# A pooling mixer and a SwiGLU layer on one core: the first layer norm's gain and bias leave VectorE's full-row pass and enter by ScalarE's copies and a later pass over rows

## The chip, the cores and the metric

One core of a Trainium2 chip. The metric is the device time of one execution in microseconds; the median of several executions is compared.

## The reference, cut to what matters

2048 tokens plus 16 learned meta tokens, 1024 features, one layer. All arithmetic is in float32.

```
m = pool_mixer(h)                                   # trailing means over 2, 4, 8, 16 tokens, w_group, w_out
h = layer_norm(ALPHA * h + m, mix_g, mix_b)         # (x - mean) * rstd * g + b
h = layer_norm(ALPHA * h + swiglu(h), ffn_g, ffn_b) # 2816 hidden features
out = h[16:]
```

## The kernel before

**Precision.** Each matmul operand is split into a rounded part ("hi", a cast by ScalarE) and a remainder ("lo", a subtraction by VectorE), and each product is three matmuls: 12 matmuls of 128x512 for four feature tiles.

**Mixer.** Four blocks of 512 tokens. `mixer_block` takes 4 chunks of hidden products (L855) and 4 of outward products (L871). ScalarE copies each hidden pair from PSUM (`stage_u`, L1093), VectorE pools it, and ScalarE and VectorE split the result again. VectorE adds `ALPHA` times the rows to the outward products (`add_rows`), takes their statistics (`aggregate`, L1441), GpSimd raises the variance to the power -0.5 (`rstd_of`, L708), and VectorE applies the norm in two passes over each row tile of 128x1024 (`apply`, L1448 and L1453). The block's four row tiles `z[:, j]` are normed in the next block, those of the last block in units 1 and 2 of the next stage. SyncE then stores them to `h_dram` (`store_h`).

**Turning.** For the gate and up products the rows must have features in partitions. TensorE transposes pairs of row tiles (`turn_part`, L843), four 128x128 at a time into a PSUM bank, and ScalarE copies each bank to SBUF (`take_turn`, L1084). Four pairs are turned in block 2, four in units 5 to 16. GpSimd makes sums of them (`pair_sums`).

**Gate and up.** The products go by a scheme of seven products for eight (`product`, L1014). There are 44 units; units 0 to 21 work on the first half of the tokens and 22 to 43 on the second. A unit is seven products, 0 to 6, of 12 matmuls each. An order written out by hand puts the other engines' work between them. Three steps must be over before TensorE goes on:

- product 2 waits for ScalarE's copy of product 0 (`b_seeded`, L1297);
- product 4 waits for VectorE's sum, called the seed below (`c_seeded`, L1610). It needs product 2 and `s5`, ScalarE's copy of product 1 (L1306);
- product 6 waits for VectorE's sum L1643 (`c22_made`), which needs product 4.

In VectorE's order the seed of unit n stands behind three remainders for the weights of unit n + 1 (`unit_lo`, L1513), and the last of these waits for a cast (`unit_hi`, L1186) that stands in ScalarE's order behind the copy `s5`:

```
                dve.wait_ge(prod_done, NP * n + 3)
                dve.wait_ge(s5_taken, n + 1)
```

GpSimd makes four differences of each unit's weights (`unit_t123`, `unit_t4`), in even units from 24 on also four 128x1024 sums (`s_forms`, L769 and L704), and up to unit 28 forms of the down weights (`tform`).

**Down.** 56 products (L1043). VectorE's `take` adds each to `z0` or `z1`, which `load_hz` and `load_hs` fill with the stored rows. The rows get `ALPHA` in VectorE's first `take` (L1678) and in two multiplications by ScalarE (L1359, L1362). GpSimd adds two of the parts (L812, L816). The last layer norm and the stores follow.

Of the kernel before, what the change touches and what calls it, by code (L numbers as in the profile page):

```python
# [30 lines left out]
def trunk(nc, x, x_t, meta_t, w_in, w_group_t, scale, w_out, mix_g, mix_b, w_gu, w_down, ffn_g, ffn_b,  # L31
# [34 lines left out]
    with ExitStack() as ctx:  # L66
# [107 lines left out]
        hs_landed = [sem("hs_landed0"), sem("hs_landed1")]  # L174
        out_stored = sem("out_stored")
# [34 lines left out]
        rstd_ready = sem("rstd_ready")  # L210
        centered = sem("centered")
# [130 lines left out]


# [15 lines left out]
        def _(sp):  # L359
# [147 lines left out]

            def load_hs(m):
# [6 lines left out]
            def store_out(r):  # L515
                zz = z0 if r < MT else z1
                sp.wait_ge(ln_applied, BLOCKS * TT + r + 1)
                sp.dma_start(out_rows[:, r, :], zz[:, r % MT].rearrange("p h t -> p (h t)")).then_inc(out_stored, 16)

            def store_last_out():  # L520
                for h in range(2):
                    sp.wait_ge(ln_applied, BLOCKS * TT + 2 * MT + h)
# [23 lines left out]
            for n, v in enumerate((mix_g, mix_b)):  # L546
                sp.dma_start(gb[:, n, :], v.partition_broadcast(P)).then_inc(gb_landed, 16)
# [80 lines left out]
            for n in range(UNITS):  # L628
# [73 lines left out]
        def _(pool):  # L702
# [19 lines left out]
            def pair_sums(pi):  # L722
                st, ss = st_of(pi), ss_of(pi)
                pool.wait_ge(turn_taken, 4 * pi + 4)
# [57 lines left out]
            pool.wait_ge(half_ready, 1)  # L782
            rstd_of(0)
# [25 lines left out]
            for m in range(MT):  # L809
                pool.wait_ge(taken, taken_by(3, m))  # L810
                pool.wait_ge(h12_scaled, m + 1)
                nc.gpsimd.tensor_tensor(z0[:, m, 1, :], z0[:, m, 1, :], z1[:, m, 1, :], ALU.add).then_inc(h12_added, 1)  # L812
                pool.wait_ge(h2_scaled, m + 1)
# [9 lines left out]
        def _(pe):  # L823
# [5 lines left out]
            def turn_part(pi, k):  # L829

                part = TT * pi + k
                if k == 0 and pi < TT:
                    pe.wait_ge(h0_landed[pi], 16)
                    pe.wait_ge(ln_applied, TT + pi + 1)
# [3 lines left out]
                if pi < TT and part >= 2:  # L838
                    pe.wait_ge(turn_taken, part - 1)
                elif pi >= TT:  # L840
                    pe.wait_ge(turn_taken, part)
# [975 lines left out]
```

## Time and profile before

| | us |
|---|---|
| median of 3 runs (1675.25 to 1678.51) | 1675.52 |
| the profiled execution, its own time | 1677.79 |
| its span | 1676.0 |
| TensorE busy | 1662.2 (99%) |
| VectorE busy | 982.6 (59%) |
| ScalarE busy | 582.3 (35%) |
| GpSimd busy | 606.1 (36%) |
| mean share of the DMA engines | some 5 tenths, 182 GB/s |
| chain that ended last | TensorE 96%, VectorE 1%, issue 1%, DMA 1%, ScalarE 1% |

Engine busy times overlap. A row of a group of instructions tells how long they ran and how long their engine was idle just before them; a row of the waits tells for whom. TensorE's granted clock was at full speed (2.4 GHz) in nearly all of the 40 slices of the span.

### The profile page before, as it was taken

Reading aid. Unit: us, or ns where it says so; the run is one execution under the profiler, and the core shown is the slowest. Engines: PE = TensorE matmul, PEld = TensorE weight load, DVE = VectorE, ACT = ScalarE, POOL = GpSimd, SP = SyncE. Lnnn points to the kernel's source line nnn. Section 1 sums busy time; section 2 is a strip of 40 time slices with the busy share of each in tenths; the row PEclk is TensorE's granted clock in tenths of the full one; section 3 lists DMA queues with packets and bytes.
Section 4 is the critical chain, followed back from the end, with each engine's and each line's share of the span. In section 5 each row is a group of like instructions: output and inputs, shape, how many; then the busy total and the mean of one; then the engine's idle time right before and its main releaser. Section 6 shows DMA issues by size and latency. Waiting matters only on the chain.

```text
span 1676.0 us, 19024 instructions
## 1 busy us (share of the span) xinstructions
PE 1662.2 (99%) x7410; PEld 1374.1 (82%) x7410; DVE 982.6 (59%) x1057; ACT 582.3 (35%) x791; POOL 606.1 (36%) x414
## 2 busy tenths in 40 slices
PE   9999999999999999999999999999999999999998
PEld 7888888888888888888878888888888888888886
DVE  6658688787744445344655564454554443568866
ACT  5332334244333333333533333333343432332320
POOL 0000024104455566565257766666632000341002
PEclk9999999999999999999999999999999999999999
DMA  9534639654445455465435676444558443554542
GB/s 358 196 104 174 224 132 323 208 211 158 155 157 165 155 195 195 152 227 179 158 108 181 207 211 202 142 138 142 197 184 306 151 157 128 193 210 175 198 147 93
DMA packets 182410, 305.67 MB, mean 182 GB/s; under 512 B 7600, under 2 KB 131632, under 8 KB 172592
## 3 DMA queue, kind: packets, MB, share of 16 engines
q1 hardware_dynamic: 142624, 272.46, 47.9%
q10 hardware_dynamic: 37520, 23.60, 4.7%
q0 software_dynamic: 2176, 8.39, 1.3%
q8 instruction: 59, 0.97, 0.2%
q14 instruction: 31, 0.25, 0.0%
HBM read 216.86 MB, written 87.56 MB: 182 GB/s over the span
## 4 chain that ended last, share of the span: by engine, by line
PE 96%; DVE 1%; issue 1%; DMA 1%; ACT 1%; POOL 0%; SPq 0%; POOLq 0%; ACTq 0%; DVEq 0%
PE acc L1014 42%; PE acc L1043 18%; PE acc L871 10%; PE acc L855 10%; PE turn L1014 7%; PE turn L1043 5%; PE acc L908 1%; PE turn L843 1%; PE acc L921 1%; DMA raw<-w_out 0%; ACT fb L1173 0%; PE acc L933 0%; DMA hs<-h_dram 0%; DMA dwr<-w_down 0%; DVE dw L1584 0%
## 5 line engine op out<-in xcount | busy, mean ns | idle before, releaser
L1014 PE MATMUL acc<-fb,wf 128*128 128x512 f32 x1584 | 364.6, 390 | 2.5 <-DVE g L1643 2.5
L1014 PE MATMUL acc<-fa,wf 128*128 128x512 f32 x1584 | 366.1, 390 | 0.0
L1014 PEld LDWEIGHTS acc<-fb,wf 128*128 128x128 f32 x1584 | 298.4, 188 | 65.0 <-issue 2.9
L1014 PEld LDWEIGHTS acc<-fa,wf 128*128 128x128 f32 x1584 | 296.1, 188 | 61.2
L1043 PE MATMUL acc<-dw,da 128*128 128x512 f32 x1386 | 315.8, 389 | 0.3 <-DVE dw L1584 0.3
L1043 PEld LDWEIGHTS acc<-dw,da 128*128 128x128 f32 x1386 | 260.0, 188 | 55.0 <-DVE dw L1584 1.0
L1513 DVE TENSOR_TENSOR wf<-wt,wf 128x512 fp32r<-128x512 f32 x132 | 125.9, 955 | 178.4 <-ACT wf L1186 178.2
L1513 DVE TENSOR_TENSOR wf<-wr,wf 128x512 fp32r<-128x512 f32 x176 | 179.8, 1030 | 80.1 <-ACT wf L1186 79.6
L1186 ACT CAST wf<-wr 128x512 fp32r<-128x512 f32 x176 | 108.7, 618 | 233.1 <-PE acc L1014 220.6
L704 POOL TENSOR_TENSOR wt<-wr,wt 128x512 f32<-128x512 f32 x88 | 128.0, 1454 | 142.7 <-DVE wf L1513 141.6
L855 PE MATMUL acc<-mov,split 128*128 128x512 f32 x768 | 176.7, 390 | 0.0
L871 PE MATMUL acc<-split,act_sb 128*128 128x512 f32 x768 | 176.2, 390 | 0.0
L871 PEld LDWEIGHTS acc<-split,act_sb 128*128 128x128 f32 x768 | 143.7, 188 | 29.7
L855 PEld LDWEIGHTS acc<-mov,split 128*128 128x128 f32 x768 | 143.5, 188 | 29.5
L1578 DVE TENSOR_TENSOR da<-dar,da 128x1408 fp32r<-128x1408 f32 x56 | 92.1, 1644 | 119.4 <-ACT da L1270 119.4
L1270 ACT CAST da<-dar 128x1408 fp32r<-128x1408 f32 x56 | 76.9, 1372 | 183.9 <-PE acc L1043 146.1
L704 POOL TENSOR_TENSOR wt<-wr 128x512 f32<-128x512 f32 x44 | 58.9, 1339 | 152.5 <-DMA wr<-w_gu 124.1
L1043 PE MATMUL turn<-dw,da 128*128 128x512 f32 x462 | 105.9, 389 | 0.0
L1043 PEld LDWEIGHTS turn<-dw,da 128*128 128x128 f32 x462 | 86.7, 188 | 18.0
L1186 ACT CAST wf<-wt 128x512 fp32r<-128x512 f32 x132 | 81.9, 621 | 52.8 <-PE acc L1014 37.5
L1374 DVE TENSOR_TENSOR split<-raw,split 128x2048 fp32r<-128x2048 f32 x31 | 72.5, 2338 | 38.9 <-ACT split L1063 38.9
L1063 ACT CAST split<-raw 128x2048 fp32r<-128x2048 f32 x31 | 59.4, 1915 | 95.3 <-PE acc L871 92.0
(115 smaller groups left out, 1588.4 us busy)
## 6 DMA issues: line engine op xcount, KB each, us to landing
wr<-w_gu SPq DMA_DIRECT2D x44, 1024.0 KB, 4.9
dar<-af_dram SPq DMA_DIRECT2D x56, 704.0 KB, 4.5
af_dram<-g ACTq DMA_DIRECT2D x33, 512.0 KB, 3.7
raw<-fold_dram SPq DMA_DIRECT2D x16, 1024.0 KB, 5.6
raw<-w_in SPq DMA_DIRECT2D x15, 1024.0 KB, 6.2
fs<-hf_dram SPq DMA_DIRECT2D x14, 1024.0 KB, 6.7
dt_raw<-w_down SPq DMA_DIRECT2D x22, 512.0 KB, 6.2
wt_dram<-dt_t SPq DMA_DIRECT2D x22, 512.0 KB, 3.6
```

The costliest lines, as they stand in the source:

```text
L704: return nc.gpsimd.tensor_tensor(out_, a, b, ALU.subtract)
L843: mm = nc.tensor.transpose(turn[:, slot, n * P:(n + 1) * P], pair_rows(pi, a)[:, kk * P:(kk + 1) * P], ident[:])
L855: mm = nc.tensor.matmul(acc[:, 2 * banks + m, :], w[:, a, k, m * P:(m + 1) * P], mov[:, k, v, :], start=k == 0 and n3 == 0, stop=k == KT - ...
L871: mm = nc.tensor.matmul(acc[:, OUT_BANK[half][j], :], act_sb[:, k0 + k, v, j * P:(j + 1) * P], w[:, a, k, :], start=first and k == 0 and n ...
L1014: mm = nc.tensor.matmul(dst, wf[:, slot, a, k, :], fa[half][i][:, v, :, k, :], start=i < 2 and k == 0 and n3 == 0, stop=k == KC - 1 and n3 ...
L1043: mm = nc.tensor.matmul(down_bank(k), da[k % 3][:, v, p, :], dw[:, slot, a, :], start=p == 0 and n3 == 0, stop=p == JF - 1 and n3 == 2)
L1063: nc.scalar.copy(split[:, slot, 0, 0:kn], raw_of(c, slot)[:, 0:kn]).then_inc(w_hi_ready, 1)
L1186: nc.scalar.copy(wf[:, (NP * n + i) % 8, 0].rearrange("p k n -> p (k n)"), w_source(n, i)).then_inc(wf_hi, 1)
L1270: nc.scalar.copy(da[k % 3][:, 0], dar[:, k % 2]).then_inc(da_hi, 1)
L1374: nc.vector.tensor_tensor(split[:, slot, 1, 0:kn], raw_of(c, slot)[:, 0:kn], f32(split[:, slot, 0, 0:kn]), ALU.subtract).then_inc(w_lo_rea ...
L1513: nc.vector.tensor_tensor(wf[:, s, 1].rearrange("p k n -> p (k n)"), w_source(n, i), f32(wf[:, s, 0]).rearrange("p k n -> p (k n)"), ALU.s ...
L1578: nc.vector.tensor_tensor(da[k % 3][:, 1], dar[:, k % 2], f32(da[k % 3][:, 0]), ALU.subtract).then_inc(da_lo, 1)
```

## The change

- `aggregate` and `rstd_of` stay. GpSimd takes two more small steps per block: mean times rstd, and its negative, `shift`.
- `apply` is gone. ScalarE writes `z * rstd + shift` in one pass for each row tile (`norm`): at the beginning of the next block, and for the last block two tiles behind `s5` in unit 1 and two in unit 2. `h_dram` now holds rows without gain and bias.
- `take_turn` brings them in: features lie in partitions there, so `mix_g` and `mix_b` are a scale and a bias per partition. One copy of 128x512 becomes two activations of 128x256.
- The stored rows are finished in units 24 to 39, one row tile of 128x1024 in each: SyncE loads it (`load_row`), VectorE multiplies by `ALPHA * g` and adds `ALPHA * b` (`finish_h`), SyncE stores it back (`store_row`). ScalarE scales the two broadcast vectors once, 128x2048, behind `s5` in unit 24.
- `ALPHA` is then in the stored rows: the two multiplications by ScalarE in the down stage go, and the first `take` is a plain addition.

```diff
@@ load_tform @@
-                else:
-                    sp.wait_ge(ln_applied, BLOCKS * TT)
@@ SyncE @@
+            def load_mgb():
+                sp.wait_ge(fa_lo, 2 * NP)
+                for n, v in enumerate((mix_g, mix_b)):
+                    sp.dma_start(mgb[:, n, :], v.partition_broadcast(P)).then_inc(mgb_landed, 16)
+            def load_row(r):
+                if r >= len(rows):
+                    sp.wait_ge(row_final, 16 * (r - 1))
+                n = r % len(rows)
+                sp.dma_start(rows[n][:], h_rows[:, r, :]).then_inc(row_landed[n], 16)
+            def store_row(r):
+                sp.wait_ge(row_ready, r + 1)
+                sp.dma_start(h_rows[:, r, :], rows[r % len(rows)][:]).then_inc(row_final, 16)
...
+                if n == ROW_UNIT0 - 1:
+                    load_mgb()
+                if 0 <= n - ROW_UNIT0 + 1 < 2 * MT:
+                    load_row(n - ROW_UNIT0 + 1)
+                if 0 <= n - ROW_UNIT0 < 2 * MT:
+                    store_row(n - ROW_UNIT0)
                 if n == UP_LAST - 3:
+                    sp.wait_ge(row_final, 16 * 2 * MT)
                     load_dw(0, 0)
@@ GpSimd, rstd_of @@
                 nc.gpsimd.tensor_tensor(rstd[:, 0:TT], var_eps[:, 0:TT], minus_half[:], ALU.pow).then_inc(rstd_ready, 1)
+                pool.wait_ge(rstd_ready, s + 1)
+                nc.gpsimd.tensor_tensor(mean_rstd[:], mv[:, 0:TT, 0], rstd[:, 0:TT], ALU.mult).then_inc(mean_scaled, 1)
+                pool.wait_ge(mean_scaled, s + 1)
+                sub(shift[:], zeros[:], mean_rstd[:]).then_inc(shift_ready, 1)
@@ ScalarE, take_turn @@
-                nc.scalar.copy(st_of(pi)[:, :, k, :], turn[:, slot, :].rearrange("p (b t) -> p b t", t=P)
-                               ).then_inc(turn_taken, 1)
+                for n, kk in enumerate((k, KC + k)):
+                    nc.scalar.activation(st_of(pi)[:, 2 * n:2 * n + 2, k, :],
+                                         turn[:, slot, 2 * n * P:2 * (n + 1) * P].rearrange("p (b t) -> p b t", t=P),
+                                         ACT.Identity, bias=mix_b_sb[:, kk:kk + 1], scale=mix_g_sb[:, kk:kk + 1]
+                                         ).then_inc(turn_taken, 1)
@@ ScalarE, mixer_block and units @@
+            def norm(s, j):
+                if j == 0:
+                    act.wait_ge(shift_ready, s + 1)
+                nc.scalar.activation(z[:, j, :], z[:, j, :], ACT.Identity, bias=shift[:, j:j + 1],
+                                     scale=rstd[:, j:j + 1]).then_inc(normed, 1)
...
+                    if b:
+                        for j in ((0, 1), (2,), (3,), ())[i]:
+                            norm(b - 1, j)
...
                 nc.scalar.copy(s5[:], bank_d).then_inc(s5_taken, 1)
+                if n == ROW_UNIT0:
+                    act.wait_ge(mgb_landed, 32)
+                    nc.scalar.mul(mgb[:], mgb[:], ALPHA).then_inc(mgb_scaled, 1)
+                if n in (1, 2):
+                    norm(LAST, 2 * (n - 1))
+                    norm(LAST, 2 * (n - 1) + 1)
@@ ScalarE, down stage @@
-                    nc.scalar.mul(z0[:, m, 1, :], z0[:, m, 1, :], ALPHA).then_inc(h12_scaled, 1)
-                    nc.scalar.mul(hs[:, m % 2], hs[:, m % 2], ALPHA).then_inc(h2_scaled, 1)
@@ VectorE @@
-            def apply(s, j):
...
-                nc.vector.scalar_tensor_tensor(out=z[:, j, :], in0=z[:, j, :], scalar=mv[:, j, 0:1], in1=gb[:, 0, :],
-                                               op0=ALU.subtract, op1=ALU.mult).then_inc(centered, 1)
...
-                nc.vector.scalar_tensor_tensor(out=z[:, j, :], in0=z[:, j, :], scalar=rstd[:, j:j + 1], in1=gb[:, 1, :],
-                                               op0=ALU.mult, op1=ALU.add).then_inc(ln_applied, 1)
+            def finish_h(r):
+                if r == 0:
+                    dve.wait_ge(mgb_scaled, 1)
+                n = r % len(rows)
+                dve.wait_ge(row_landed[n], 16 * (r // len(rows) + 1))
+                nc.vector.tensor_tensor(rows[n][:], rows[n][:], mgb[:, 0, :], ALU.mult).then_inc(row_gained, 1)
+                dve.wait_ge(row_gained, r + 1)
+                nc.vector.tensor_tensor(rows[n][:], rows[n][:], mgb[:, 1, :], ALU.add).then_inc(row_ready, 1)
@@ VectorE, units, behind the fourth remainder for unit n + 1 @@
-                if n in (1, 2):
-                    apply(LAST, 2 * (n - 1) + 1)
+                if 0 <= n - ROW_UNIT0 < 2 * MT:
+                    finish_h(n - ROW_UNIT0)
```

`ROW_UNIT0` is 24. Line numbers below in rows of the changed kernel are its own: L1242 is the cast that was L1186, L1371 the copy `s5` that was L1306, L1569 the remainder that was L1513, L1672 the seed that was L1610.

ScalarE in unit 1, before: from the copy of product 0 to the three casts that are due between products 2 and 5.

```order
L1297 COPY acc<-acc 128x512
L1186 CAST wf<-wt 128x512
L1306 COPY s_92<-turn 128x512
L1186 CAST wf<-wt 128x512
L1186 CAST wf<-wr 128x512 x3
```

The same place in the changed kernel:

```order
L1362 COPY acc<-acc 128x512
L1242 CAST wf<-wt 128x512
L1371 COPY s_92<-turn 128x512
L1248 ACTIVATE z<-z,shift,rstd 128x1024 x2
L1242 CAST wf<-wt 128x512
L1242 CAST wf<-wr 128x512 x3
```

Two norms of a row tile have come between the copy `s5` and the cast on which VectorE's third remainder waits.

ScalarE in unit 24, in the changed kernel:

```order
L1362 COPY acc<-acc 128x512
L1323 DMA af_dram<-g 128x8x128
L1242 CAST wf<-wt 128x512
L1371 COPY s_92<-turn 128x512
L1374 ACTIVATE mgb<-mgb 128x2048
L1242 CAST wf<-wt 128x512
```

The scaling of the two vectors stands at the same place.

VectorE from the two remainders ahead of the seed of unit 24 to those ahead of the seed of unit 25, in the changed kernel (`rows_107` is the first row buffer):

```order
L1569 TENSOR_TENSOR wf<-wt,wf 128x512 x2
L1672 TENSOR_TENSOR acc<-s_92,acc 128x512
L1569 TENSOR_TENSOR wf<-wr,wf 128x512
L1703 TENSOR_TENSOR g<-s_92,acc 128x512
L1569 TENSOR_TENSOR wf<-wr,wf 128x512
L1634 TENSOR_TENSOR rows_107<-rows_107,mgb 128x1024
L1636 TENSOR_TENSOR rows_107<-rows_107,mgb 128x1024
L1569 TENSOR_TENSOR wf<-wr,wf 128x512
L1569 TENSOR_TENSOR wf<-wt,wf 128x512
L1569 TENSOR_TENSOR wf<-wr,wf 128x512
L1569 TENSOR_TENSOR wf<-wt,wf 128x512 x2
L1672 TENSOR_TENSOR acc<-s_92,acc 128x512
```

Only the two rows L1634 and L1636 are new; five remainders stand between them and the next seed.

## Rows read from the trace of the kernel before

**Rows 1.** Every wait of TensorE (engine line <- releaser: us, times, longest)
```profile
PE acc L1014 <- DVE g L1643: 2.5, 1, 2.5
PE acc L908 <- DVE split L1467: 1.9, 2, 1.4
PE turn L886 <- POOL act_sb L776: 1.3, 1, 1.3
PE acc L1043 <- DVE dw L1584: 0.3, 1, 0.3
```

**Rows 2.** Busy time by stretch (columns: us, PE, PEld, DVE, ACT, POOL, clock, DMA)
```profile
1662.00:1676.00 14.00, 6.30 (x28) 4.88 (x26) 7.46 (x12) 0.00 (x0) 3.04 (x2) 0.91 0.20 75
```

**Rows 3.** Groups by line and form (count, busy us, mean ns, idle before)
```profile
L1063 ACT CAST split<-raw 128x2048 fp32r<-128x2048 f32 x31 | 59.4, 1915 | 95.3 <-PE acc L871 92.0 <-DMA raw<-w_in 2.3 <-ACT st_mix L1084 1.0
...
L1448 DVE SCALAR_TENSOR_TENSOR z<-z,mv,gb 128x1024 f32<-128x1024 f32 x16 | 23.5, 1472 | 0.0
...
L1407 DVE TENSOR_TENSOR sums<-sums 128x1024 f32<-128x1024 f32 x12 | 15.8, 1319 | 0.4
...
L1084 ACT COPY st_mix<-turn 128x512 f32<-128x512 f32 x16 | 8.7, 590 | 3.6 <-PE turn L843 3.6
L1362 ACT ACTIVATE hs<-hs 128x1024 f32<-128x1024 f32 x8 | 8.5, 1061 | 14.0 <-DMA hs<-h_dram 14.0
...
L708 POOL TENSOR_TENSOR rstd<-var_eps,minus_half 128x4 f32<-128x4 f32 x4 | 7.3, 1821 | 234.5 <-DVE var_eps L1443 234.5
```

**Rows 4.** DMA issues (count, KB, median us to landing)
```profile
h_dram<-z SPq DMA_DIRECT2D x16, 512.0 KB, 4.7
```

**Rows 5.** Timeline of VectorE, block 2 (start us, us, ...)
```profile
224.36 1.28 DVE L1453 SCALAR_TENSOR_TENSOR z<-z,rstd,gb 128x1024 f32<-128x1024 f32 x1 [0.91 <-POOL rstd L708]
```

**Rows 6.** Timeline of ScalarE, block 2
```profile
228.24 1.01 ACT L1093 COPY stage<-acc 128x1024 f32<-128x1024 f32 x1 [8.91 <-PE acc L855]
...
236.92 1.05 ACT L1084 COPY st_mix<-turn 128x512 f32<-128x512 f32 x2
```

**Rows 7.** Timeline of TensorE, block 2
```profile
239.82 0.27 PE L843 MATMUL turn<-ident,z 128*128 128x128 f32 x1
```

**Rows 8.** Timeline of TensorE, products 1 and 2 of unit 1
```profile
420.39 2.88 PE L1014 MATMUL turn<-fa,wf 128*128 128x512 f32 x12
423.11 16.48 PE L1014 MATMUL acc<-fa,wf 128*128 128x512 f32 x72
```

**Rows 9.** Timeline of ScalarE, unit 1
```profile
423.31 0.59 ACT L1306 COPY s<-turn 128x512 f32<-128x512 f32 x1 [1.61 <-PE turn L1014]
423.79 0.63 ACT L1186 CAST wf<-wt 128x512 fp32r<-128x512 f32 x1
```

**Rows 10.** Timeline of VectorE, units 1 and 2
```profile
424.45 1.02 DVE L1513 TENSOR_TENSOR wf<-wt,wf 128x512 fp32r<-128x512 f32 x1 [1.93 <-ACT wf L1186]
426.03 0.70 DVE L1610 TENSOR_TENSOR acc<-s,acc 128x512 f32<-128x512 f32 x1 [0.56 <-PE acc L1014]
...
446.39 2.31 DVE L1448 SCALAR_TENSOR_TENSOR z<-z,mv,gb 128x1024 f32<-128x1024 f32 x1
```

**Rows 11.** Timeline of ScalarE, unit 24
```profile
873.31 0.59 ACT L1306 COPY s<-turn 128x512 f32<-128x512 f32 x1 [1.55 <-PE turn L1014]
```

**Rows 12.** Timeline of TensorE, product 2 on of unit 26
```profile
911.19 9.00 PE L1014 MATMUL acc<-fb,wf 128*128 128x512 f32 x39
```

**Rows 13.** Timeline of VectorE from the end of unit 25 into unit 26
```profile
906.66 0.69 DVE L1513 TENSOR_TENSOR wf<-wr,wf 128x512 fp32r<-128x512 f32 x1 [1.96 <-ACT wf L1186]
...
909.87 2.50 DVE L1513 TENSOR_TENSOR wf<-wt,wf 128x512 fp32r<-128x512 f32 x1 [1.92 <-ACT wf L1186]
912.53 2.64 DVE L1513 TENSOR_TENSOR wf<-wt,wf 128x512 fp32r<-128x512 f32 x1 [0.17 <-ACT wf L1186]
915.10 0.68 DVE L1610 TENSOR_TENSOR acc<-s,acc 128x512 f32<-128x512 f32 x1
```

**Rows 14.** Timeline of GpSimd, unit 24
```profile
872.30 2.85 POOL L704 TENSOR_TENSOR sx<-sa,g 128x1024 f32<-128x1024 f32 x1
```

More of the change, by code:

```diff
@@ L135, in trunk @@
         hs = at("hs", Z0, [P, 2, D])
+        mgb = at("mgb", N0, [P, 2, D])
+        rows = [at(f"rows{n}", V0 + n * 4 * KB, [P, D]) for n in range(2)]
         ident = sb("ident", [P, P])
         scale_sb = sb("scale_sb", [P, KT])
+        mix_g_sb = sb("mix_g_sb", [P, KT])
+        mix_b_sb = sb("mix_b_sb", [P, KT])
+        zeros = sb("zeros", [P, TT])
+        mean_rstd = sb("mean_rstd", [P, TT])
+        shift = sb("shift", [P, TT])
         stats = sb("stats", [P, 2 * MT, HALVES, 6])
@@ L174, in trunk @@
         hs_landed = [sem("hs_landed0"), sem("hs_landed1")]
+        mix_gb_landed = sem("mix_gb_landed")
+        mgb_landed = sem("mgb_landed")
+        row_landed = [sem(f"row_landed{n}") for n in range(len(rows))]
+        row_final = sem("row_final")
         out_stored = sem("out_stored")
@@ L210, in trunk @@
         rstd_ready = sem("rstd_ready")
+        zeros_ready = sem("zeros_ready")
+        mean_scaled = sem("mean_scaled")
+        shift_ready = sem("shift_ready")
+        normed = sem("normed")
+        mgb_scaled = sem("mgb_scaled")
+        row_gained = sem("row_gained")
+        row_ready = sem("row_ready")
         centered = sem("centered")
@@ L545, in _ @@
             load_chunk(c_in(0, 3), 1, w_in[3])
-            for n, v in enumerate((mix_g, mix_b)):
-                sp.dma_start(gb[:, n, :], v.partition_broadcast(P)).then_inc(gb_landed, 16)
+            for tile, v in ((mix_g_sb, mix_gt), (mix_b_sb, mix_bt)):
+                sp.dma_start(tile[:], v).then_inc(mix_gb_landed, 16)
             sp.wait_ge(group_lo_ready, 3)
@@ L723, in pair_sums @@
                 st, ss = st_of(pi), ss_of(pi)
-                pool.wait_ge(turn_taken, 4 * pi + 4)
+                pool.wait_ge(turn_taken, 2 * (4 * pi + 4))
                 if pi:
@@ L782, in _ @@
             pool.wait_ge(half_ready, 1)
+            nc.gpsimd.memset(zeros[:], 0.0).then_inc(zeros_ready, 1)
+            pool.wait_ge(zeros_ready, 1)
             rstd_of(0)
@@ L810, in _ @@
                 pool.wait_ge(taken, taken_by(3, m))
-                pool.wait_ge(h12_scaled, m + 1)
+                pool.wait_ge(hz_landed[m], 16)
                 nc.gpsimd.tensor_tensor(z0[:, m, 1, :], z0[:, m, 1, :], z1[:, m, 1, :], ALU.add).then_inc(h12_added, 1)
-                pool.wait_ge(h2_scaled, m + 1)
+                pool.wait_ge(hs_landed[m % 2], 16 * (m // 2 + 1))
                 pool.wait_ge(h12_added, m + 1)
@@ L838, in turn_part @@
                 if pi < TT and part >= 2:
-                    pe.wait_ge(turn_taken, part - 1)
+                    pe.wait_ge(turn_taken, 2 * (part - 1))
                 elif pi >= TT:
-                    pe.wait_ge(turn_taken, part)
+                    pe.wait_ge(turn_taken, 2 * part)
                 for n, (a, kk) in enumerate(((1, k), (0, k), (0, KC + k), (1, KC + k))):
@@ L1439, in aggregate @@
             def aggregate(s):
+                if s:
+                    dve.wait_ge(normed, s * TT)
                 for j in range(TT):
@@ L1535, in mixer_block @@
                         d_lo(b, i - 1)
-                    if not first:
-                        for j in ((0, 1), (), (2,), (3,))[i]:
-                            apply(b - 1, j)
                     if b == LAST and i == 2:
@@ L1670, in _ @@
             up_out(2 * JF - 1, 1, bank(UP_LAST, 1))
-            dve.wait_ge(gb_landed, 64)
+            dve.wait_ge(gb_landed, 32)
+            dve.wait_ge(normed, BLOCKS * TT)
             def take(k):
@@ L1677, in take @@
                     dve.wait_ge(hz_landed[m], 16)
-                    nc.vector.scalar_tensor_tensor(out=z0[:, m, 0, :], in0=z0[:, m, 0, :], scalar=ALPHA, in1=down_bank(k),
-                                                   op0=ALU.mult, op1=ALU.add).then_inc(taken, 1)
+                    nc.vector.tensor_tensor(z0[:, m, 0, :], z0[:, m, 0, :], down_bank(k), ALU.add).then_inc(taken, 1)
                     return
@@ L1797 @@
         "mix_b": np.ascontiguousarray(inputs["ln_mix_b"][0]),
+        "mix_gt": lay(inputs["ln_mix_g"], (kt, P), (1, 0)),
+        "mix_bt": lay(inputs["ln_mix_b"], (kt, P), (1, 0)),
         "w_gu": np.ascontiguousarray(blocks(w_gu).transpose(1, 2, 3, 0, 4, 5)),
```

37 lines of the change are left out of this document (15 added, 22 removed).

## The prediction

> **What bounds the kernel now.** I read the waits of TensorE first. There are five in all [rows 1]: 1.9 us and 1.3 us at the start, 2.5 us in unit 22 and 0.3 us at the head of the down stage. The last 14 us hold 14.00 - 6.30 = 7.7 us without TensorE, the final row and its store [rows 2]. Waits and tail together come to 13.7 us, and TensorE is idle for 1676.0 - 1662.2 = 13.8 us of the span. So nothing else is idle time: from unit 0 to the last product TensorE runs on but for 2.8 us. The number of matmuls and transposes does not change. VectorE's passes that the change removes lie beside TensorE's work, so their removal is worth nothing by itself. What can change the time is a new wait of TensorE. The reader is to look for places where a moved step stands ahead of something that TensorE needs.
>
> Everything below is compared with the profiled execution, 1677.79 us (span 1676.0). It is 2.27 us above the median of the runs, 1675.52; I add the difference that I work out to the median. A measurement of this kernel can tell about 0.2%, 3.35 us, from no change.
>
> **The change part by part.**
>
> *Removed from VectorE:* 16 row tiles in two passes, the first of 1472 ns on average [rows 3] and the second like it (one took 1.28 us [rows 5]), some 46 us over four blocks. Cover: TensorE never waited for them. Worth 0.
>
> *Norms by ScalarE, blocks 1 to 3.* No row shows this operation; the nearest is ScalarE's 128x1024 scaling, 1.06 us [rows 3]. Two of them now stand ahead of the copy of the block's first hidden pair and wait for `shift`. In block 2 VectorE had its rstd at 224.36 [rows 5]. GpSimd's two extra steps on 128x4 are bounded below by almost nothing, and above by its power on 128x4, 1.82 us each [rows 3]. `shift` is then there between 224.4 and 228.0, and the norms end between 226.5 and 230.1. The copy stood at 228.24, where TensorE's products ended [rows 6]. So it is late by 0 to 1.9 us. VectorE, without its own passes, is free in time to pool the pair. Who waits in the end: ScalarE's copies of the turned rows, at 236.92, two in 1.05 us [rows 6]; TensorE writes the first of the two banks again at 239.82 [rows 7]. A copy of 128x512 takes 0.59 us [rows 3]; its two halves between 0.6 and 1.2 us. The first bank is free between 237.5 and 240.0, the second between 238.1 and 241.2, which is wanted some 0.5 us after the first. TensorE waits 0 to 0.9 us. The small steps should be nearer to nothing than to the power, so I take 0. The other pairs have no wait for `shift`.
>
> *Norms in units 1 and 2.* TensorE begins product 1 of unit 1 at 420.39 and product 2 at 423.11 [rows 8], so a product takes 2.72 us, and product 4 is due at 423.11 + 5.44 = 428.55. Its chain: `s5` at 423.31 for 0.59 us, then at once the cast, 0.63 us [rows 9], then VectorE's third remainder and the seed [rows 10]. Now two norms of 1.06 us stand between `s5` and the cast. The cast ends at 423.90 + 2.12 + 0.63 = 426.65. The remainder takes 1.02 us [rows 10], and up to 2.64 us beside GpSimd [rows 13]; the seed 0.70 us. The seed ends at 428.4 or, at worst, at 430.0. TensorE waits 0 to 1.4 us. I take the unit's own row, which leaves 0.2 us, and put 0.1 us on each of the two units for semaphores. What ScalarE has queued behind it (casts of unit 2) has most of a unit's time.
>
> *Scaling of the two vectors in unit 24.* The nearest row is a cast of 128x2048, 1.91 us [rows 3]. `s5` starts at 873.31 [rows 11]; by the same step as in unit 1, product 4 is due 5.24 us later, at 878.55. The cast ends at 873.90 + 1.91 + 0.63 = 876.44, the remainder between 877.5 and 879.1, the seed between 878.2 and 879.8. GpSimd is in its long sums here [rows 14], so the remainder is nearer to the long value. TensorE waits 0 to 1.2 us; I take 0.6. The vectors are asked for in unit 23, so their transfer is no issue.
>
> *The row passes in units 24 to 39.* A plain VectorE operation with both inputs in SBUF and 128x1024 takes 1.32 us [rows 3], and a pass of the same size took 2.31 us with GpSimd beside it [rows 10]. So a pair costs 2.6 to 4.6 us. It stands behind the sum that product 6 needs, so the first to feel it is the next unit's seed. The tight seeds are those of even units, for GpSimd's sums slow the remainders ahead of them. From the end of unit 25 on VectorE is idle for 1.96 + 1.92 + 0.17 = 4.05 us ahead of the seed of unit 26 [rows 13]. That seed ends at 915.78. Product 2 begins at 911.19 [rows 12], so product 4 is due at 916.63: 0.85 us more. In all 4.9 us, against 4.6 at worst. The passes cost 0, narrowly. GpSimd's last difference waits for VectorE's last remainder and slips with it; it stands with its long sums in an even unit later than before, and ScalarE's gate behind them, but TensorE's own sums come later still.
>
> *Transfers.* 16 loads and 16 stores of 512 KB are added, two broadcasts of as much are moved, two tiny loads stand in their old place. A store of this size lands in 4.7 us [rows 4]; each row is loaded a unit (19 us) ahead. In SyncE's order the new store waits for VectorE's pass, but the next weight load behind it waits for a later remainder anyway. 0.
>
> *Down stage.* Sixteen scalings by ScalarE go (eight of them of 1.06 us [rows 3]); GpSimd waited for them and TensorE for neither. The first `take` has the same shape as before. 0. The tail is untouched.
>
> **Sum:** 0.1 + 0.1 + 0.6 = +0.8 us; bounds 0 and 0.9 + 1.4 + 1.4 + 1.2 = 4.9. Forecast: 1675.52 + 0.8 = 1676.3 us, 1678.6 for an execution like the profiled one.
>
> **The rivals.**
>
> 1. *Unit 22's wait goes.* Its 2.49 us are a wait for VectorE [rows 1], and VectorE's load is what the change touches. Against it: the row passes begin in unit 24 and the norms ended in unit 2, so VectorE's own order there is the same. It would give 1675.5 - 2.5 = 1673.0, still within 0.2%; only with some of the start's waits would it be more.
>
> 2. *The late seeds add up (slower).* All four places of the bounds at their upper end: 1675.5 + 4.9 = 1680.4. For it: each chain leaves only tenths of a microsecond. Against it: the upper ends take GpSimd beside every remainder. The point from which it decides is a third remainder of more than 1.2 us in units 1 and 2.
>
> 3. *VectorE's row pass is held for a whole GpSimd operation (slower).* GpSimd's longest operations last 2.85 us [rows 14]. If each of the two passes waits for one, the pair takes 2 x (1.32 + 2.85) = 8.3 us against the 4.9 that are free: 3.4 us of wait in each of even units 26 to 40, eight times, 27 us: 1675.5 + 0.8 + 27 = 1703. It decides from a pair of 4.9 us on. For it: the remainders at 909.87 and 912.53 took 2.5 and 2.64 us where others took 0.69 [rows 13]. Against it: the pair stands at the end of a unit, the long sums at the beginning of even ones.
> The Trainium skill ("SBUF — State Buffer", "Who interferes with whom") says that a VectorE instruction with two SBUF inputs contends with a GpSimd instruction that reads SBUF, and that the pair of ports is held for a whole instruction rather than shared. The trace agrees as far as it goes: 2.31 us against 1.28 for one shape.
>
> 4. *VectorE is not relieved at all.* If the added pairs take 4.6 us each, 74 us come for the 46 that go, and the change only moves hidden work to a later stage. The time is then the same as before, 1675.5.
>
> **How the numbers follow.** Forecast 0.80 (sums from 0 to 3.3 us, no change that can be told). Rival 1 0.06, a third of it with more than 3.35 us of gain. Rival 2 0.07. Rival 3 0.05. Rival 4 0.02, no change either. Faster: 0.02. Slower: 0.07 + 0.05 = 0.12. Same: 0.86. For the range I leave out rival 3 and the far part of rival 1: from 1674.0 to 1680.4.
>
> **What would show each step.** TensorE's waits would list the seed in units 1, 2 and 24 with some tenths each, unit 22 with about 2.5 us as before, and no row for the copies of turned rows. VectorE's busy time should fall little: 46 us go, 16 pairs of 2.6 to 4.6 us, 42 to 74 us, come. ScalarE should be up by some 10 us. The row passes should read near 1.3 us, those beside GpSimd above 2. I am wrong if TensorE waits in each even unit from 26 on, or in block 2, or if the wait of unit 22 is gone.

## The result, and the profile after

| | before | changed |
|---|---|---|
| median, us (20 runs each, taken together) | 1676.61 (1675.02 to 1678.57) | 1680.15 (1677.53 to 1683.45) |
| ratio, 95% interval | | 1.0020 (1.0014 to 1.0026) |
| profiled execution, us | 1677.79 | 1677.53 |

The change makes the kernel slower by 3.3 us (2.3 to 4.4). The forecast was 1676.3, its range ended at 1680.4. The profiled execution of the changed kernel is the fastest of its 20, 2.6 us under the median: its trace shows the places of the loss, but it is no longer than that of the kernel before (span 1675.7 against 1676.0 us). A trace of usual length is that of e3 below.

TensorE's waits behind the mixer in that trace, to be held against [rows 1], and the same in its timeline (start, us, matmuls, idle before):

```profile
PE acc L1064 <- DVE acc L1672: 2.0, 3, 1.1
PE acc L1064 <- DVE g L1703: 1.6, 1, 1.6
```

```profile
843.44 5.71 PE L1064 MATMUL acc<-fb,wf 128*128 128x512 f32 x24 [1.63 <-DVE g L1703]
...
876.57 11.16 PE L1064 MATMUL acc<-fb,wf 128*128 128x512 f32 x48 [0.23 <-DVE acc L1672]
...
972.70 11.16 PE L1064 MATMUL acc<-fb,wf 128*128 128x512 f32 x48 [0.64 <-DVE acc L1672]
...
1031.57 11.16 PE L1064 MATMUL acc<-fb,wf 128*128 128x512 f32 x48 [1.09 <-DVE acc L1672]
```

The wait of unit 22 is there, 1.63 us (2.49 in [rows 1]). New are three waits for the seed (now L1672), in units 24, 29 and 32: 0.23, 0.64 and 1.09 us. None is in units 1 and 2, and none in block 2. The wait of 0.3 us in the down stage is gone.

Busy times from unit 24 to the end of the units (us, then TensorE, weight loads, VectorE, ScalarE, GpSimd, clock, DMA share, GB/s), before and in the changed kernel:

```profile
860.00:1249.00 389.00, 389.00 (x1718) 322.11 (x1717) 204.39 (x217) 131.04 (x226) 248.45 (x144) 1.00 0.56 169
```

```profile
860.00:1249.00 389.00, 387.04 (x1704) 319.17 (x1703) 273.73 (x247) 130.95 (x225) 260.44 (x144) 1.00 0.67 211
```

VectorE has 69 us more to do here and GpSimd, with the same instructions, takes 12 us longer.

The row passes and the transfers, to be held against [rows 3] and [rows 4] (count, busy us, mean ns; then transfers with the median us to landing):

```profile
L1634 DVE TENSOR_TENSOR rows<-rows,mgb 128x1024 f32<-128x1024 f32 x16 | 37.5, 2344 | 0.0
...
L1636 DVE TENSOR_TENSOR rows<-rows,mgb 128x1024 f32<-128x1024 f32 x16 | 27.8, 1737 | 0.6
```

```profile
af_dram<-g ACTq DMA_DIRECT2D x33, 512.0 KB, 6.0
...
rows<-h_dram SPq DMA_DIRECT2D x16, 512.0 KB, 7.5
```

A pair of row passes takes 2.34 + 1.74 = 4.1 us on average, near the upper end of my 2.6 to 4.6. The average hides what matters: the pair took 5.6 us (3.42 + 2.20) in units 26, 28 and 30, above that end, and 2.4 us (1.21 + 1.23) in unit 27. The norm takes 1.24 us (I had 1.06), the scaling 1.92 (1.91), GpSimd's small step 0.23 us (between nothing and 1.82). In all VectorE is busy for 1001.8 us and ScalarE for 603.0, against 982.6 and 582.3 before. ScalarE's stores of the gate products, 3.7 us to landing before, now take 6.0:

```profile
af_dram<-g ACTq DMA_DIRECT2D x33, 512.0 KB, 3.7
```

In unit 1 of the changed kernel ScalarE does what was worked out from [rows 9]: the two norms stand between `s5` and the cast. VectorE then took 0.69 us for the remainder, not 1.02, and TensorE did not wait.

```profile
423.09 0.59 ACT L1371 COPY s<-turn 128x512 f32<-128x512 f32 x1 [1.61 <-PE turn L1064]
423.58 2.38 ACT L1248 ACTIVATE z<-z,shift,rstd 128x1024 f32<-128x1024 f32 x2
425.86 0.60 ACT L1242 CAST wf<-wt 128x512 fp32r<-128x512 f32 x1
```

What is quite new stands among the waits of units 23 to 30. Before the change neither ScalarE's gate nor VectorE's sum ever waited for GpSimd there:

```profile
ACT g L1313 <- POOL sx L746: 14.3, 3, 6.1
...
ACT wf L1242 <- POOL g L807: 5.6, 2, 3.7
DVE g L1703 <- POOL sx L746: 5.4, 1, 5.4
```

In unit 30 of this trace that sum also waited 3.3 us for ScalarE's store of gate products to land; the traces of the kernel before and of e3 have no such wait.

One instance, unit 28. GpSimd's first difference of the weights waits for their load, which SyncE now issues behind a row's load and store, at 930.70 us and not at 927.71. First the kernel before, then the changed kernel. TensorE is 1.9 us further on in the changed kernel's trace here, so against TensorE's work the lateness is larger by that much:

```profile
936.26 1.29 POOL L704 TENSOR_TENSOR wt<-wr 128x512 f32<-128x512 f32 x1
```

```profile
939.89 1.82 POOL L746 TENSOR_TENSOR wt<-wr 128x512 f32<-128x512 f32 x1 [2.27 <-DMA wr<-w_gu]
```

GpSimd's second long sum ended at 954.0 us before and ends at 957.0 now. What follows in the changed kernel: GpSimd's first two long sums, ScalarE's gate, VectorE's sum L1703, the row passes, the two remainders and the seed of unit 29. Three timelines:

```profile
952.29 2.39 POOL L817 TENSOR_TENSOR sx<-g 128x1024 f32<-128x1024 f32 x1
954.64 2.39 POOL L746 TENSOR_TENSOR sx<-sa,g 128x1024 f32<-128x1024 f32 x1
```

```profile
957.12 0.60 ACT L1313 ACTIVATE g<-acc 128x512 f32<-128x512 f32 x1 [6.11 <-POOL sx L746]
```

```profile
957.16 0.69 DVE L1703 TENSOR_TENSOR g<-s,acc 128x512 f32<-128x512 f32 x1 [5.43 <-POOL sx L746]
...
959.99 3.42 DVE L1634 TENSOR_TENSOR rows<-rows,mgb 128x1024 f32<-128x1024 f32 x1
963.45 2.19 DVE L1636 TENSOR_TENSOR rows<-rows,mgb 128x1024 f32<-128x1024 f32 x1
...
969.57 2.38 DVE L1569 TENSOR_TENSOR wf<-wt,wf 128x512 fp32r<-128x512 f32 x2
971.87 0.68 DVE L1672 TENSOR_TENSOR acc<-s,acc 128x512 f32<-128x512 f32 x1
```

The gate and the sum start as GpSimd's second sum ends, at 957.0. VectorE gets to its row passes at 959.99 and then needs 3.42 and 2.19 us for them, beside GpSimd. ScalarE's cast for the second of the two remainders also waited for GpSimd, 1.3 us. The seed of unit 29 starts at 971.87, and TensorE, idle for 0.64 us, goes on at 972.70.

The longest seed wait, 1.09 us in unit 32, shows the same lateness. The weights land late there too (GpSimd's first difference starts at 1015.71 us, before at 1009.60), its long sums start at 1025.07 in place of 1022.27, and they meet the two remainders ahead of the seed. These took 0.83 and 1.26 us before and now 5.10 us together:

```profile
1025.72 5.10 DVE L1569 TENSOR_TENSOR wf<-wt,wf 128x512 fp32r<-128x512 f32 x2 [1.17 <-ACT wf L1242]
```

### The profile page after: what moved, and what is told of

It reads as the page before. It is cut to its first block, busy times and chain, and to the rows that moved or that the text cites. A ratio compares the mean times of both kernels' runs of the same rounds, so it can differ in the third digit from the quotient of the medians.

```text
span 1675.7 us, 19103 instructions
## 1 busy us (share of the span) xinstructions
PE 1661.5 (99%) x7410; PEld 1373.3 (82%) x7410; DVE 1001.8 (60%) x1057; ACT 603.0 (36%) x824; POOL 616.6 (37%) x423
## 4 chain that ended last, share of the span: by engine, by line
PE 94%; DVE 2%; issue 1%; DMA 1%; POOL 1%; ACT 1%; SPq 0%; POOLq 0%; DVEq 0%; ACTq 0%
PE acc L1064 39%; PE acc L1093 19%; PE acc L921 10%; PE acc L905 10%; PE turn L1064 7%; PE turn L1093 6%; DVE wf L1569 1%; PE acc L958 1%; PE turn L893 1%; DMA wr<-w_gu 1%; PE acc L971 0%; DMA raw<-w_out 0%; DVE rows L1634 0%; POOL wt L746 0%; DVE rows L1636 0%
## 5 line engine op out<-in xcount | busy, mean ns | idle before, releaser
L1569 DVE TENSOR_TENSOR wf<-wt,wf 128x512 fp32r<-128x512 f32 x132 | 134.4, 1022 | 151.7 <-ACT wf L1242 151.4
L1569 DVE TENSOR_TENSOR wf<-wr,wf 128x512 fp32r<-128x512 f32 x176 | 181.0, 1033 | 57.8 <-ACT wf L1242 57.3
L1242 ACT CAST wf<-wr 128x512 fp32r<-128x512 f32 x176 | 108.8, 618 | 219.8 <-PE acc L1064 205.7
L746 POOL TENSOR_TENSOR wt<-wr 128x512 f32<-128x512 f32 x44 | 63.2, 1437 | 157.9 <-DMA wr<-w_gu 125.2
L1242 ACT CAST wf<-wt 128x512 fp32r<-128x512 f32 x132 | 81.7, 620 | 59.7 <-PE acc L1064 37.9
```

Of the source, the lines that this page charges most:

```text
L746: return nc.gpsimd.tensor_tensor(out_, a, b, ALU.subtract)
L1242: nc.scalar.copy(wf[:, (NP * n + i) % 8, 0].rearrange("p k n -> p (k n)"), w_source(n, i)).then_inc(wf_hi, 1)
L1569: nc.vector.tensor_tensor(wf[:, s, 1].rearrange("p k n -> p (k n)"), w_source(n, i), f32(wf[:, s, 0]).rearrange("p k n -> p (k n)"), ALU.s ...
```

## The experiments

Each group is compared with runs of the kernel before on its own chip; that median was 1677.1 to 1677.2 us in the first three groups and 1676.3 in the last. e1 to e4 share their runs of it, e5 to e8 theirs, and e9 to e11 theirs.

**e1: no passes.**

```diff
-                if 0 <= n - ROW_UNIT0 < 2 * MT:
-                    finish_h(n - ROW_UNIT0)
@@ store_row
-                sp.wait_ge(row_ready, r + 1)
+                sp.wait_ge(row_landed[r % len(rows)], 16 * (r // len(rows) + 1))
```

> The changed kernel without VectorE's two passes over each stored row tile; loads, stores and the scaling of the two vectors stay (so the stored rows lack ALPHA, gain and bias). Theory P (the 3.5 us are TensorE's waits for seeds that the passes, 65 us of VectorE in units 24 to 39, make late, directly and through the queue of GpSimd): back to the kernel before, ratio to it 0.999 to 1.001, and no waits for L1672's counterpart behind unit 24. Theory T (the added 16.8 MB make weight loads land later, so that GpSimd, and behind it ScalarE's cast, are late): stays at 1.0015 to 1.0025 with seed waits between units 26 and 40. Theory M (the moves of the norm and of the scaling to ScalarE cost it): stays above 1.001 with no such waits.

Measured: 1678.51 us, ratio 1.0006 (0.9997 to 1.0014). By the ratios the passes are the larger part of the loss, some 2 of the 3.3 us (1.0020 less 1.0006), but seed waits did not go:

```profile
PE acc L1064 <- DVE g L1703: 2.6, 1, 2.6
...
PE acc L1064 <- DVE acc L1672: 1.3, 2, 1.0
```

The larger, 1.03 us, is in unit 30. The chain of work ahead of it (start, us, what) runs through the transfers and GpSimd:

```profile
971.29 10.14 DMA wr<-w_gu
...
981.50 1.74 POOL wt L746
...
986.32 1.26 POOL g L807
```

The weight load, behind a row's load and store, takes 10.14 us. GpSimd starts its differences when it lands; its product L807 follows and ScalarE's cast waits for that. The two remainders now fall together with GpSimd's long sums, 5.74 us for both:

```profile
988.79 5.74 DVE L1569 TENSOR_TENSOR wf<-wt,wf 128x512 fp32r<-128x512 f32 x2 [3.03 <-ACT wf L1242]
```

**e2: passes, but no transfers of rows.** Two row tiles are loaded, none is stored, and the passes work on them again and again.

```diff
-                if 0 <= n - ROW_UNIT0 + 1 < 2 * MT:
+                if 0 <= n - ROW_UNIT0 + 1 < len(rows):
                     load_row(n - ROW_UNIT0 + 1)
-                if 0 <= n - ROW_UNIT0 < 2 * MT:
-                    store_row(n - ROW_UNIT0)
```

> The changed kernel with the 32 passes, but only two row tiles loaded and none stored: the passes work on the same two buffers again and again (the stored rows lack ALPHA, gain and bias). Theory P: the loss stays, ratio to the kernel before 1.001 to 1.002, seed waits stay, the first pass still reads about 2.3 us. Theory T: the loss goes, ratio 0.999 to 1.0005, no seed waits. If loss needs both, both this run and the one without passes are near 1.000.

Measured: 1680.14 us, ratio 1.0012 (1.0003 to 1.0021). By the medians the loss stays, by the ratio two fifths of it go; the times fell into two groups, 1676.4 to 1677.6 (5 runs) and 1680.1 to 1683.3 (7). The trace is of a run of the first group. Seed waits stay, three in all, 0.23 us in unit 24 and:

```profile
972.91 11.15 PE L1062 MATMUL acc<-fb,wf 128*128 128x512 f32 x48 [0.64 <-DVE acc L1672]
...
993.12 11.14 PE L1062 MATMUL acc<-fb,wf 128*128 128x512 f32 x48 [0.91 <-DVE acc L1672]
```

So neither half alone is the cause, and the passes without the transfers still lose. The two halves, 1.0006 and 1.0012, add up to about the whole, 1.0020.

**e5: no row work at all.** As e1, and also without `load_mgb`, `load_row`, `store_row` and the scaling of `mgb`.

> The changed kernel with the whole row work left out: no passes, no loads and stores of rows, no scaling of the two vectors (the stored rows lack ALPHA, gain and bias); norms and turned copies stay on ScalarE. Theory R (all of the loss is the row work, its passes and its transfers each a part): ratio to the kernel before 0.9995 to 1.0005, no seed wait at all behind unit 22. Theory M (part of it is in the norms or the two-piece copies): stays at 1.0006 or above as without the passes, 1678.5 against 1677.1.

Measured: 1676.74 us, ratio 0.9995 (0.9986 to 1.0003). From unit 0 to the last product one wait is left, that of unit 22:

```profile
PE acc L1057 <- DVE g L1693: 2.6, 1, 2.6
```

The norms on ScalarE and the copies in two pieces cost nothing; theory M is out. All of the loss is in the row work. The norms' gain for VectorE is worth nothing that can be told either.

**One stretch without the scatter.** The time from product 1 of unit 24 to product 1 of unit 43, 19 units, is free of what varies from run to run in the mixer and in unit 22. It is 361.76 us in all five traces without row work: before, e4, e5, e8 and e12. With row work it is 363.14 (e9, below), 363.59 (e1), 364.36 (e2), 364.95 (the changed kernel) and 365.45 (e3, next; its edit is in unit 22 and its run, 1680.84 us, one of usual length). The ends of the stretch in the kernel before and in e3, then e3's seed waits:

```profile
870.39 2.88 PE L1014 MATMUL turn<-fb,wf 128*128 128x512 f32 x12
...
1232.15 2.88 PE L1014 MATMUL turn<-fb,wf 128*128 128x512 f32 x12
```

```profile
870.84 2.88 PE L1064 MATMUL turn<-fb,wf 128*128 128x512 f32 x12
...
1236.29 2.88 PE L1064 MATMUL turn<-fb,wf 128*128 128x512 f32 x12
```

```profile
PE acc L1064 <- DVE acc L1672: 2.6, 4, 1.1
```

All of e3's 3.69 us lie in the four units with a seed wait: 24, 29, 30 and 32 are longer than a unit's 19.04 us by 0.48, 0.77, 1.09 and 1.35 us, and the others are not. No slow matmuls stand behind these waits, 48 take 11.13 to 11.16 us. Against this stands a gain: from the first product of the down stage to the end of the span the kernel before takes 427.5 us, the changed kernel and e3 426.4, e5 426.7. 3.7 - 1.1 = 2.6 us in e3; its span is 3.0 us longer than that of the kernel before, and the rest lies ahead of unit 24, most of it in the mixer.

**e3 and e4: the new form first, in unit 22,** in the changed kernel (e3) and in the kernel before (e4).

```diff
-        FORM_LO.update({(HALF_UNITS, 3): NP + 5, (HALF_UNITS, 4): NP + 6})
+        FORM_LO.update({(HALF_UNITS, 3): NP + 5})
...
                     new_form(n, 3)
+                    if n == HALF_UNITS:
+                        form_lo(NP + 6)
                     unit_lo(n + 1, 3)
```

> The changed kernel with VectorE's order altered at one place: in unit 22 the remainder of the last new form comes ahead of a weight remainder of unit 23 instead of behind it. Before the change TensorE waited 2.49 us there and its next 24 matmuls took 7.28 us where 24 take 5.7 after a shorter wait, so the place cost about 4 us; in the profiled run of the changed kernel it waited 1.63 us. If that wait comes from VectorE's order: shorter by 1.6 us or more there, and 1.6 to 4 us less than the changed kernel, ratio to the kernel before 0.999 to 1.001. If it is set by ScalarE's cast or by the form's load: no difference from the changed kernel, 1.002.

> The kernel before with that same alteration in unit 22 alone. If the wait comes from VectorE's order: ratio 0.9975 to 0.999 (1.6 to 4 us less), TensorE's wait in unit 22 below 1 us and no stretch of slow matmuls behind it. If not: 1.000 and the same 2.5 us. If variation of this place from run to run is what spreads the times of the kernel before (1675.0 to 1678.6), its spread shrinks too.

Measured: 1680.43 us, 1.0018 (1.0009 to 1.0027), and 1677.14 us, 1.0001 (0.9993 to 1.0010). No gain, and e4's spread (1676.1 to 1680.4) did not shrink. VectorE's timeline and TensorE's in e4 show why:

```profile
837.59 5.59 DVE L1506 TENSOR_TENSOR fb<-fs,fb 128x2048 fp32r<-128x2048 f32 x2 [0.51 <-ACT fb L1173]
843.11 1.74 DVE L1513 TENSOR_TENSOR wf<-wr,wf 128x512 fp32r<-128x512 f32 x1
844.77 0.68 DVE L1645 TENSOR_TENSOR g<-s,acc 128x512 f32<-128x512 f32 x1
```

```profile
845.60 5.69 PE L1014 MATMUL acc<-fb,wf 128*128 128x512 f32 x24 [2.56 <-DVE g L1645]
```

The two forms end at 843.1, when product 6 was due (845.60 - 2.56 = 843.04). The weight remainder, 1.74 us, still stands between them and the sum.

**e8 and e12: that remainder behind the sum,** in the kernel before; e12 is the same kernel again.

```diff
                     new_form(n, 3)
-                    unit_lo(n + 1, 3)
+                    if n != HALF_UNITS:
+                        unit_lo(n + 1, 3)
...
                 nc.vector.tensor_tensor(dst, s5[:], bank(n, 1), ALU.add).then_inc(c22_made, 1)
+                if n == HALF_UNITS:
+                    unit_lo(n + 1, 3)
```

> The kernel before; in unit 22 one weight remainder moved behind the sum on which TensorE waits (with the swap alone the wait stayed at 2.56 us, since that remainder, 1.74 us, still stood ahead of the sum; the two new forms ended 0.1 us after product 6 was due). If VectorE's order sets this wait: 0.6 to 1.0 us instead of 2.5, no slow matmuls behind it, ratio 0.998 to 0.9995. If the forms, not the order, set it: 2.5 us and 1.000.

> The kernel before with the weight remainder of unit 22 behind the sum, once more, since its first interval (0.9982 to 1.0000) touched no change. If the gain of 1.5 to 1.8 us is real: ratio 0.9985 to 0.9995 again, and TensorE's wait in unit 22 near 0.8 us with no slow matmuls behind it. If it was chance: 1.000. Its spread should be narrower at the top than that of the kernel before, whose slowest runs have the lowest mean clock.

Measured: 1675.36 us, 0.9991 (0.9982 to 1.0000), and 1675.53 us, 0.9993 (0.9984 to 1.0002). The wait shrank as expected, from 2.49 us to 0.77 and, in e12, 0.78:

```profile
843.97 5.72 PE L1014 MATMUL acc<-fb,wf 128*128 128x512 f32 x24 [0.77 <-DVE g L1644]
```

The times agree with a gain of 1 to 2 us, but neither interval excludes no change. Both point the same way: an estimate of the two together, if they are independent, is 0.9992 with some 0.0006 on either side, and that would exclude no change. The slowest of these 22 runs took 1677.75 us; the kernel before reached 1679.8 beside each. By its medians this is the fastest version that was tried.

**e6 and e9: row work only in units 29 to 39,** 11 tiles; e9 also loads and scales the two vectors in unit 23.

```diff
-        ROW_UNIT0 = HALF_UNITS + 2
+        ROW_UNIT0 = HALF_UNITS + 7
@@ e9 alone: load_mgb and its scaling
-                if n == ROW_UNIT0 - 1:
+                if n == HALF_UNITS + 1:
```

> The changed kernel with row tiles 0 to 10 only, in units 29 to 39; tiles 11 to 15 stay unfinished. Units 24 to 28, where GpSimd has the down weights' forms beside its long sums, have no row work. Theory G (what makes the seeds late is GpSimd's queue, full in units 24 to 28: there ScalarE's gate and VectorE's sum wait 14 and 5 us for its long sums in the changed kernel's trace and never before): no such waits in units 24 to 28, ratio 1.000 to 1.0008. Theory V (VectorE's own backlog in each unit, wherever): loss in proportion, 11 of 16 tiles, ratio 1.0012 to 1.0015.

Measured in e6: 1684.23 us, 1.0039 (1.0025 to 1.0052), 5 runs. The vectors had just been asked for, and ScalarE stood behind them in unit 29:

```profile
ACT mgb L1374 <- DMA mgb<-mix_b: 7.0, 1, 7.0
```

```profile
980.32 13.75 PE L1064 MATMUL acc<-fb,wf 128*128 128x512 f32 x48 [6.07 <-DVE acc L1672]
```

> As the run with row work only in units 29 to 39 (11 tiles, five stay unfinished), but the two vectors are loaded and scaled in unit 23. In that run ScalarE waited 7.0 us for the second vector in unit 29, TensorE 6.07 us behind it, and its next 48 matmuls took 13.75 us in place of 11.2: 8.6 us of my own making, and no other seed wait. Theory G (only the row work of units 24 to 28 costs anything, through GpSimd's queue): ratio 0.9995 to 1.0006, no seed wait. Theory V: 1.001 or more, seed waits in units 29 to 39.

Measured in e9: 1678.47 us, 1.0006 (0.9997 to 1.0016). TensorE's waits in the units:

```profile
994.09 11.17 PE L1064 MATMUL acc<-fb,wf 128*128 128x512 f32 x48 [1.09 <-DVE acc L1672]
```

In the trace neither ScalarE's gate nor VectorE's sum waits for GpSimd's sums any more, so those waits do belong to units 24 to 28. But one seed wait stays, in unit 30. By time the two theories are not told apart: 11 sixteenths of 0.0020 is 0.0014, inside the interval. Theory G in its narrow form (only units 24 to 28) falls with the wait of unit 30.

**e7 and e10: the complete row work, placed otherwise.** Both scale the vectors at the end of ScalarE's unit 23.

```diff
                 if n + 2 < UNITS:
                     load_unit(n + 2)
+                if 0 <= n - ROW_UNIT0 - 1 < 2 * MT:
+                    store_row(n - ROW_UNIT0 - 1)
@@ VectorE, ahead of the sum
+                if 0 <= n - ROW_UNIT0 < 2 * MT and not gate:
+                    finish_h(n - ROW_UNIT0)
@@ VectorE, the old place, odd units
+                if 0 <= n - ROW_UNIT0 < 2 * MT and not gate:
+                    bias_h(n - ROW_UNIT0)
@@ VectorE, behind the last remainder, even units
+                    if 0 <= n - ROW_UNIT0 < 2 * MT and gate:
+                        finish_h(n - ROW_UNIT0)
+                        bias_h(n - ROW_UNIT0)
```

Here `finish_h` is the first pass alone and `bias_h` the second. In e7 `load_row(n - ROW_UNIT0)` stands behind the weight load too, in the row's own unit.

> The changed kernel complete, its row work placed otherwise: loads and stores of rows behind the next weight load in SyncE's order, not ahead of it; in even units both passes behind the last remainder, in odd units the first ahead of the sum L1703 and the second where it was; the scaling of the vectors at the end of unit 23, not behind the copy s5 of unit 24. Theory G: weight loads land earlier and the last remainder of even units is not late, so GpSimd's queue keeps its times of before; ratio 0.9998 to 1.0008, the wait in unit 24 gone. Theory V (the work is too much wherever it stands): 1.0015 or more, as the changed kernel.

Measured in e7: 1679.57 us, 1.0019 (1.0010 to 1.0028). No seed wait was left, but one wait for the sum of unit 29, where VectorE had waited 5.7 us for a row:

```profile
980.37 8.60 PE L1064 MATMUL acc<-fb,wf 128*128 128x512 f32 x24 [2.92 <-DVE up L1708]
```

> The complete spread version with row loads a unit ahead again (in the first one VectorE waited 5.7 us for a row in unit 29, and TensorE 2.92 us behind it; there was no seed wait). Stores stay behind the weight load. Theory G: ratio 0.9998 to 1.0007, no waits of TensorE from unit 24 on of more than 0.5 us in all. Theory V: 1.0015 or more as before.

Measured in e10: 1678.96 us, 1.0007 (0.9999 to 1.0016). Two places in TensorE's timeline:

```profile
844.00 5.70 PE L1064 MATMUL acc<-fb,wf 128*128 128x512 f32 x24 [1.04 <-DVE g L1708]
...
993.31 12.77 PE L1064 MATMUL acc<-fb,wf 128*128 128x512 f32 x48 [2.16 <-DVE acc L1675]
```

One seed wait of 2.16 us in unit 30 stays, with a slow stretch behind it: more than the 0.5 us that theory G allowed, so this run speaks against theory G too. The interval no longer excludes the time of the kernel before. It would take more runs to say whether it beats the changed kernel.

**e11: e10 with the remainder of unit 22 behind the sum.**

> The run before it plus the one remainder of unit 22 behind the sum L1643's counterpart, which took 1.8 us off the kernel before (1675.4 against 1677.2). If the two add: 1.5 to 2 us below the run before it, ratio to the kernel before 0.9985 to 0.9998; TensorE's wait in unit 22 below 1 us. Without the row work's loss it would equal the altered kernel before, 1675.4.

Measured: 1677.04 us, 1.0000 (0.9991 to 1.0009), 1.9 us under e10 by the medians.

```profile
843.63 5.71 PE L1064 MATMUL acc<-fb,wf 128*128 128x512 f32 x24 [0.73 <-DVE g L1709]
...
993.19 11.15 PE L1064 MATMUL acc<-fb,wf 128*128 128x512 f32 x48 [2.19 <-DVE acc L1675]
```

With both edits the complete change stands level with the kernel before. The kernel before with the edit of unit 22 alone, 1675.4 and 1675.5 us, is still under it.

## Why the prediction was right or wrong

The measured time lies in the range, at its upper end, and near rival 2. The sum was +0.8 us, the loss 3.3. That the range held is partly luck: its upper end was added up from four other places, and the price of the row passes, put at 0, was partly paid back by a gain in the down stage, also put at 0. By step:

- *What bounds the kernel:* right. TensorE runs on but for named waits, and VectorE's removed passes were worth nothing that can be told: e5, which has all the moves and no row work, is at 0.9995.
- *Norms in block 2:* right. The small steps took 0.23 us, no wait.
- *Norms in units 1 and 2:* I put 0.2 us, 0 was measured. A norm took 1.24 us and not 1.06, but the remainder took 0.69.
- *Scaling in unit 24:* I took 0.6 us. The wait was 0.23 in every version that had the scaling there (the changed kernel, e1, e2, e3), and it lengthened the unit by 0.5.
- *The row passes: this is the step that failed.* "The passes cost 0, narrowly." The term was 0, but behind unit 24 the stretch grew by 2.7 us in the changed kernel's trace and by 3.2 in e3's, for passes and transfers together. The case that I worked out, the pair of unit 25 ahead of the seed of unit 26, came true: 3.5 us and no wait there. The error was to check that one case with everything else where it was before. The pairs of units 26, 28 and 30 took 5.6 us, over my 4.6, and the late seeds were those of units 29, 30 and 32, not of all even units. In the traces the passes move the last remainder, so the weight load and GpSimd's queue start later; GpSimd's sums then meet the next passes (3.42 us at 959.99) and remainders (5.10 us in unit 32). I had named GpSimd's slipping queue and dismissed it with "TensorE's own sums come later still". In unit 28 the sum L1703 itself waited 5.4 us for it.
- *Transfers:* I put 0. By time e1 and e5 differ by the transfers and the scaling, 1678.5 against 1676.7 us; the intervals overlap, so this is a tendency. The traces show it: 363.59 against 361.76 us in the stretch without the scatter, 0.5 of it by the scaling. The mechanism in e1 is a weight load of 10.14 us behind a row's load and store.
- *Tail and down stage:* no new wait, as forecast, but a gain of 1.1 us that I had put at 0. TensorE's wait for a remainder at L1584 is gone in every trace with the new down stage; in the kernel before the 198 matmuls around it take 45.67 us from their start to the next product (1487.83 to 1533.50), where 198 others take 44.88. That is 0.8 us. The other 0.3 lie in the tail, and nothing shows why.
- *Busy times:* VectorE's rose by 19 us, where I let it fall little or stay, and ScalarE's by 21, where I had some 10.

Rival 3 fell as priced: no wait stands in each even unit. Its mechanism was there, though. The pairs of units 26, 28 and 30 took 5.6 us, above the 4.9 from which it was to decide, and the pass at 959.99 ended 1.1 us after GpSimd's sum beside it (959.60, for 2.73 us), where a pass alone takes 1.2. Rival 2 had the right place, seeds, but its chance of 0.07 was low: I put 0.80 on sums up to 3.3 us, the measured loss is at that edge. Its mechanism, GpSimd beside every remainder in units 1, 2 and 24, was not what made the seeds of units 29 to 32 late. Rival 1 fell: the wait of unit 22 is in every trace, 0.7 to 2.6 us long. Rival 4's premise came true, since 65 us of passes came for the 46 that went, but the time did not stay.

What stays open: how exactly the loss divides between passes and transfers, since the ratios of e1 and e2 are each uncertain by 0.0009; why a seed wait of 1.1 to 2.2 us stays in unit 30 when the row work is placed otherwise (e9, e10, e11); and what the share of unit 22 is in a usual run of the changed kernel, where its own trace shows 1.63 us and e3's 2.50 with slow matmuls behind.

## What to carry to other kernels

Idle time of an engine in a trace is no room for new work if another engine's queue starts where that idle time ends: follow the moved instruction's signal through every queue (here remainder, weight load, GpSimd's differences, ScalarE's cast, remainder) before pricing it at nothing. An average over a group can hide the one pair that is too long. When the scatter of whole runs is as large as the effect, compare a stretch of the traces that the scatter leaves alone. Of a wait for an instruction, look at what stands between it and the last thing that it really needs: one 1.7 us instruction behind the sum rather than ahead of it cut a wait that reordering the work ahead had not touched. And where a bound engine idles for a microsecond or two, count what follows the wait too.

## What the runs showed of the hardware

A wait of TensorE can cost more than its own length. Each of e3's seed waits lengthened its unit by 0.25 to 0.28 us more than the idle time that the trace gives for it (for instance 0.77 for 0.50). Some waits cost more still. In the kernel before 24 matmuls behind the wait of unit 22 took 7.28 us, in the changed kernel behind 1.63 us 5.71 (above):

```profile
844.24 7.28 PE L1014 MATMUL acc<-fb,wf 128*128 128x512 f32 x24 [2.49 <-DVE g L1643]
```

The granted clock of 820 to 860 us was 0.96 in the first and 1.00 in the second: part of that stretch went at the lower of its two levels, 1.2 in place of 2.4 GHz. It does not follow from the wait's length alone. Behind 2.56 us in e4 the matmuls took 5.69 us; e10 and e11 waited 2.16 and 2.19 us at the seed of unit 30, and their next 48 matmuls took 12.77 and 11.15. In the units no trace has it behind a wait of 1.63 us or less. This goes with the spread of the times: 35 runs of the kernel before with mean clock 0.999 average 1676.3 us (10 runs), with 0.997 1678.6 (10 runs); of the changed kernel 1678.8 (7 runs) and 1681.9 (4 runs). It is a tendency only: in e12 the three runs at 0.997 average 1675.7 us and the four at 0.999 1675.4.

VectorE's and GpSimd's operations slowed each other: the same remainder of 128x512 took 0.69 us alone and 2.9 beside GpSimd's 128x1024 sums, and such a sum took 2.4 us or up to 2.87. "SBUF — State Buffer" of the Trainium skill ("Who interferes with whom") has the port as held for a whole instruction; the trace agrees, since the 5.74 us of e1's two remainders are about as long as the two sums beside them (2.40 and 2.85 us) and what was left to do.
